# Norm sums of the mixers as wide float32r products, with root and reciprocal on 128x512 tiles

## What is computed

```python
# recurrence: o is (B, S, 4 heads, 128); the mean runs over the 128 values of a head
o = o * lax.rsqrt(jnp.mean(o * o, axis=-1, keepdims=True) + EPS)
o = o.reshape(bsz, s, A_WIDTH) * norm_g.astype(f32) * jax.nn.silu(g.astype(f32))

# attention: o is (B, S, 512); the mean runs over all 512 values of a token
return rmsnorm(o, norm_g).astype(q.dtype)
```

## Time and profile before

| | |
|---|---|
| median of 3 runs | 2477.68 us (2477.02 to 2479.18) |
| span of the profiled execution | 2476.5 us |
| TensorE busy | 2442.7 us, 99% |
| VectorE busy | 1336.4 us, 54% |
| ScalarE busy | 859.4 us, 35% |
| GpSimd busy | 254.0 us, 10% |

### The profile page before, as it was taken

How to read it: one execution, slowest core, us unless ns; L and a number is a source line. 1 busy time by engine, 2 the same in 40 slices (tenths; PEclk the granted TensorE clock), 3 DMA queues, 4 the chain that set the end, 5 groups by cost and what they waited for, 6 DMA issues and landing times.

```text
span 2476.5 us, 33433 instructions
## 1 busy us (share of the span) xinstructions
PE 2442.7 (99%) x11896; PEld 2022.3 (82%) x11896; DVE 1336.4 (54%) x2063; ACT 859.4 (35%) x1325; POOL 254.0 (10%) x237
## 2 busy tenths in 40 slices
PE   6999999999999999999999999999999999999998
PEld 5888888888888888888888888888888888888887
DVE  4665544555666554545556655455556665545433
ACT  4444422233344432223334453222334444222211
POOL 1220100000122100000012220000002122000000
PEclk9999999999999999999999999999999999999999
DMA  4222333333322233333331223333333223333332
GB/s 111 68 69 77 95 101 93 107 104 103 111 64 75 77 102 93 96 107 111 96 117 52 77 86 94 101 93 103 108 104 111 58 73 92 94 101 93 93 94 85
DMA packets 400998, 228.39 MB, mean 92 GB/s; under 512 B 11648, under 2 KB 388480, under 8 KB 400896
## 3 DMA queue, kind: packets, MB, share of 16 engines
q1 hardware_dynamic: 398592, 218.68, 29.8%
q10 hardware_dynamic: 2304, 8.39, 0.8%
HBM read 218.65 MB, written 8.39 MB: 92 GB/s over the span
## 4 chain that ended last, share of the span: by engine, by line
PE 97%; DMA 1%; DVE 1%; SPq 0%; issue 0%; ACT 0%; ACTq 0%; DVEq 0%
PE M L462 27%; PE M L464 27%; PE M L463 27%; PE X L544 2%; PE M L566 1%; PE X L607 1%; PE X L462 1%; PE X L463 1%; PE X L464 1%; PE X L620 1%; PE X L555 1%; PE X L480 1%; PE X L590 1%; PE X L469 1%; PE X L614 1%; DMA xs<-in_x_dram 1%
## 5 line engine op out<-in xcount | busy, mean ns | idle before, releaser
L1088 DVE TENSOR_TENSOR wlo<-raw,whi 128x1024 fp32r<-128x1024 f32 (+1 forms) x392 | 477.2, 1217 | 975.7 <-ACT whi L793 975.7
L462 PE MATMUL M<-uhi,whi 128*128 128x512 f32 x2112 | 833.7, 395 | 5.4 <-issue 3.8
L464 PE MATMUL M<-uhi,wlo 128*128 128x512 f32 x2112 | 823.9, 390 | 0.0
L463 PE MATMUL M<-ulo,whi 128*128 128x512 f32 x2112 | 823.6, 390 | 0.0
L793 ACT ACTIVATE whi<-raw 128x1024 fp32r<-128x1024 f32 (+1 forms) x392 | 408.5, 1042 | 1089.8 <-PE M L464 1079.9
L462 PEld LDWEIGHTS M<-uhi,whi 128*128 128x128 f32 x2112 | 397.3, 188 | 90.2 <-issue 9.1
L464 PEld LDWEIGHTS M<-uhi,wlo 128*128 128x128 f32 x2112 | 397.2, 188 | 84.2
L463 PEld LDWEIGHTS M<-ulo,whi 128*128 128x128 f32 x2112 | 397.7, 188 | 81.3 <-issue 1.0
L462 PE MATMUL M<-ahi,whi 128*128 128x512 f32 x832 | 331.4, 398 | 0.0
L464 PE MATMUL M<-ahi,wlo 128*128 128x512 f32 x832 | 328.4, 395 | 0.0
L463 PE MATMUL M<-alo,whi 128*128 128x512 f32 x832 | 328.3, 395 | 0.0
(11 more groups left out here) (175 smaller groups left out, 2164.5 us busy)
## 6 DMA issues: line engine op xcount, KB each, us to landing
raw<-in_w_in_dram SPq DMA_DIRECT2D x88, 512.0 KB, 3.9
raw<-in_w_gate_dram SPq DMA_DIRECT2D x88, 512.0 KB, 3.8
raw<-in_w_up_dram SPq DMA_DIRECT2D x88, 512.0 KB, 3.8
raw<-in_w_down_dram SPq DMA_DIRECT2D x64, 512.0 KB, 3.6
raw<-in_w_out_dram SPq DMA_DIRECT2D x32, 512.0 KB, 3.6
raw<-in_w_down_dram SPq DMA_DIRECT2D x32, 384.0 KB, 3.1
xs<-in_x_dram SPq DMA_DIRECT2D x32, 256.0 KB, 4.1
out_dram<-os ACTq DMA_DIRECT2D x16, 512.0 KB, 2.6
```

The lines of the kernel that those rows point to most:

```text
L462: mm(bank, whi[s][:, kb, :], hi, start=first, stop=False)
L463: mm(bank, whi[s][:, kb, :], lo, start=False, stop=False)
L464: return mm(bank, wlo[s][:, kb, :], hi, start=False, stop=last)
L1088: V.tensor_tensor(wlo[s][:, 0:nb, :], raw[s][:, 0:nb, :], whi[s][:, 0:nb, :].bitcast(F32), ALU.subtract).then_inc(s_lo[s], 1)
```

## The change

The two forms of the norm product are replaced. The squares are split in a high part (a float32r copy by ScalarE) and a low part (the difference, by VectorE), and two float32r products of a 128x128 tile of ones with them leave each token's sum on all 128 partitions of the bank: `sums_wide`. Nothing has to be spread any more. Root and reciprocal therefore work on 128x512 instead of 128x4, into `sqo` for the heads and `sroot` for the attention, and the factor is read from SBUF by the product with `gate` or `oT`. For a head the root stays in its slot and the reciprocal moves to the start of the next, before the product. For the attention the parts are made in slot 21 and sums, root and reciprocal stand in slot 22. The parts lie on memory that is free at that time (`gu`, `qT[1]`, `qT[2]`).

```diff
-            def spread(bank, factors, done):
-
-                for b in range(TB):
-                    last = mm(bank[:, b * P:(b + 1) * P], factors[:, b:b + 1].broadcast_to([P, P]), ident[:, :],
-                              start=True, stop=True)
-                last.then_inc(done, 1)
+            def sums_wide(bank, hi, lo, done):
+
+                mm(bank[:, :], ones_r[:, :], hi[:, :], start=True, stop=False)
+                mm(bank[:, :], ones_r[:, :], lo[:, :], start=False, stop=True).then_inc(done, 1)
...
             def head_sum(it, a):
-                pe.wait_ge(s_sq, it * HEADS + a + 1)
+                pe.wait_ge(s_sqlo, it * HEADS + a + 1)
                 pe.wait_ge(s_st, it * NCH * HEADS + NCH * a + NCH)
-                sums(X[3], sqo, s_asum)
-
-            def head_mul(it, a):
-                pe.wait_ge(s_arr, it * HEADS + a + 1)
-                spread(X[3], hrnrm, s_amul)
+                sums_wide(X[3], sqh, sql, s_asum)
...
-                    if slot == SWA_SUM:
-                        pe.wait_ge(s_oacc, it * (PAIRS - 1) + PAIRS - 1)
-                        sums(X[1], qT[0], s_ssum)
                     if slot == SWA_MUL:
-                        pe.wait_ge(s_srr, it + 1)
-                        spread(X[1], srnrm, s_smul)
+                        pe.wait_ge(s_sslo, it + 1)
+                        sums_wide(X[1], ssh, ssl, s_ssum)
...
             def output(it, a):
-                act.wait_ge(s_o, it * HEADS + a + 1)
+                n = it * HEADS + a
+                act.wait_ge(s_o, n + 1)
                 if a:
-                    act.wait_ge(s_asum, it * HEADS + a)
+                    act.wait_ge(s_ya, n)
                 A(sqo[:, :], X[2][:, :], ACT.Square).then_inc(s_sq, 1)
+                act.wait_ge(s_sq, n + 1)
+                A(sqh[:, :], sqo[:, :], ACT.Copy).then_inc(s_sqhi, 1)
...
-                A(hnrm[:, :], X[3][:, 0:TB], ACT.Sqrt, scale=1.0 / P, bias=epst[:, 0:1]).then_inc(s_aroot, 1)
+                A(sqo[:, :], X[3][:, :], ACT.Sqrt, scale=1.0 / P, bias=epst[:, 0:1]).then_inc(s_aroot, 1)
...
                     if slot == SWA_SUM:
+                        act.wait_ge(s_oacc, it * (PAIRS - 1) + PAIRS - 1)
+                        A(ssh[:, :], qT[0][:, :], ACT.Copy).then_inc(s_sshi, 1)
+                    if slot == SWA_MUL:
                         act.wait_ge(s_ssum, it + 1)
-                        A(snrm[:, :], X[1][:, 0:TB], ACT.Sqrt, scale=1.0 / (PAIRS * P),
+                        A(sroot[:, :], X[1][:, :], ACT.Sqrt, scale=1.0 / (PAIRS * P),
                           bias=epst[:, 0:1]).then_inc(s_sroot, 1)
...
+            def square_lo(it, a):
+                n = it * HEADS + a
+                dve.wait_ge(s_sqhi, n + 1)
+                if a:
+                    dve.wait_ge(s_asum, n)
+                V.tensor_tensor(sql[:, :], sqo[:, :], sqh[:, :].bitcast(F32), ALU.subtract).then_inc(s_sqlo, 1)
+
+            def head_mul(it, a):
                 n = it * HEADS + a
                 dve.wait_ge(s_aroot, n + 1)
-                if a:
-                    dve.wait_ge(s_amul, n)
-                V.reciprocal(hrnrm[:, :], hnrm[:, :]).then_inc(s_arr, 1)
-
-            def head_mul(it, a):
-                n = it * HEADS + a
-                dve.wait_ge(s_amul, n + 1)
+                V.reciprocal(sqo[:, :], sqo[:, :]).then_inc(s_arr, 1)
+                dve.wait_ge(s_arr, n + 1)
                 dve.wait_ge(s_y1, n + 1)
-                V.tensor_tensor(gate[a % 2][:, :], gate[a % 2][:, :], X[3][:, :], ALU.mult).then_inc(s_ya, 1)
+                V.tensor_tensor(gate[a % 2][:, :], gate[a % 2][:, :], sqo[:, :], ALU.mult).then_inc(s_ya, 1)
...
                     if slot == SWA_SUM:
+                        dve.wait_ge(s_sshi, it + 1)
+                        V.tensor_tensor(ssl[:, :], qT[0][:, :], ssh[:, :].bitcast(F32), ALU.subtract).then_inc(s_sslo, 1)
+                    if slot == SWA_MUL:
                         dve.wait_ge(s_sroot, it + 1)
-                        V.reciprocal(srnrm[:, :], snrm[:, :]).then_inc(s_srr, 1)
-                    if slot == SWA_MUL:
-                        dve.wait_ge(s_smul, it + 1)
+                        V.reciprocal(sroot[:, :], sroot[:, :]).then_inc(s_srr, 1)
+                        dve.wait_ge(s_srr, it + 1)
                         swa_mul(it, 0)
...
-                    for offset, step in ((KEYS, keys), (UPDATE, update), (OUTPUT, output), (NORM_SUM, head_sum)):
+                    for offset, step in ((KEYS, keys), (UPDATE, update), (OUTPUT, output), (OUTPUT, square_lo)):
```

More of the change, by code:

```diff
@@ L172, in block_program @@
         state = sb("state", [P, HEADS, P])
+        gu_at = (nc.sbuf_base + 31) // 32 * 32
         gu = [sb(f"gu{i}", [P, T]) for i in range(2)]
+        sqh, sql = (nc.alloc_sbuf_tensor_at(f"sq_part{i}", [P, T], F32R, offset=gu_at + 4 * T * i) for i in range(2))
         dist = sb("dist", [P, 2 * BLOCK])
@@ L177, in block_program @@
         ones = sb("ones", [P, P])
+        ones_r = sb("ones_r", [P, P], F32R)
         causal = sb("causal", [P, P])
@@ L215, in block_program @@
         gate = [tile(f"gate{i}") for i in range(2)]
+        q_at = free_tiles[:PAIRS]
         qT = [tile(f"qT{i}") for i in range(PAIRS)]
+        ssh, ssl = (nc.alloc_sbuf_tensor_at(f"ss_part{i}", [P, T], F32R, offset=q_at[1 + i]) for i in range(2))
+        sroot = qT[3]
         pr = [tile(f"pr{i}") for i in range(2)]
@@ L289, in block_program @@
         s_oacc = sem("s_oacc")
+        s_sshi = sem("s_sshi")
+        s_sslo = sem("s_sslo")
         s_ssum = sem("s_ssum")
@@ L292, in block_program @@
         s_srr = sem("s_srr")
-        s_smul = sem("s_smul")
         s_yb = sem("s_yb")
@@ L323, in block_program @@
         s_y1 = sem("s_y1")
+        s_sqhi = sem("s_sqhi")
+        s_sqlo = sem("s_sqlo")
         s_asum = sem("s_asum")
@@ L326, in block_program @@
         s_arr = sem("s_arr")
-        s_amul = sem("s_amul")
         s_ya = sem("s_ya")
@@ L347, in block_program @@
         s_osb = sem("s_osb")
-        INI, DST = 10, 4
+        INI, DST = 11, 4
         block = ctx.enter_context(nc.Block())
@@ L671, in slots @@
                             key_turn(it, HEADS - 1)
-                    a = head_at(slot, NORM_MUL)
-                    if a is not None:
-                        head_mul(it, a)
                     a = head_at(slot, UPDATE)
@@ L1241, in swa_mul @@
                 V.scalar_tensor_tensor(out=oT[p][:, :], in0=oT[p][:, :], scalar=gb[:, p:p + 1],
-                                       in1=X[1][:, :], op0=ALU.mult, op1=ALU.mult).then_inc(s_yb, 1)
+                                       in1=sroot[:, :], op0=ALU.mult, op1=ALU.mult).then_inc(s_yb, 1)
             def swa_lo(it, p):
@@ L1458, in _ @@
             G.memset(causal[:, :], -1.0).then_inc(s_ini, 1)
+            G.memset(ones_r[:, :].bitcast(F32), 1.0).then_inc(s_ini, 1)
             G.iota(dist[:, :].bitcast(I32), [[1, 2 * BLOCK]], base=-BLOCK, channel_multiplier=-1).then_inc(s_ini, 1)
-            pool.wait_ge(s_ini, 7)
+            pool.wait_ge(s_ini, 8)
             G.affine_select(out=causal[:, :], in_=causal[:, :], compare_op=ALU.is_ge, fill=0.0, base=0,
@@ L1465, in _ @@
             G.tensor_copy(dist0[:, :], dist[:, :].bitcast(I32)).then_inc(s_ini, 1)
-            pool.wait_ge(s_ini, 9)
+            pool.wait_ge(s_ini, 10)
             G.memset(causal[0:CHUNK, CHUNK:P], 0.0).then_inc(s_ini, 1)
@@ L1478, in _ @@
             pool.wait_ge(s_dst, 4)
-            pool.wait_ge(s_ini, 10)
+            pool.wait_ge(s_ini, 11)
             def copy(out, in_):
```

5 lines of the change are left out of this document (removed).

## The result

The changed kernel takes 2493.44 us (median of 4 runs, 2490.63 to 2497.53); the kernel before, on the same chip, 2477.80 (2477.02 to 2479.18). The ratio is 1.0062, with a 95% interval of 1.0048 to 1.0076: slower, by 15.6 us, where 22.8 were forecast. The profiled execution took 2490.63 us, its span is 2488.8 (12.3 more than before) and its mean granted clock 0.989, where the kernel before had 0.997.

What follows compares the result with a forecast made beforehand. TensorE's own work was taken to bound the kernel, busy 2442.7 of 2476.5 us. Savings of 26.8, waits of 4 x 9.4 and clock of 12.0 gave +22.8 us: 2500.5 us, range 2485 to 2508.

Steps and rivals of the forecast that it cites:

- What is taken off TensorE: Norm sums and spreading: two float32r products replace them, saving 1.34 us per norm, 6.7 per superblock, 26.8 in all.
- Rival (c): Product with ones runs in several passes like fp32, so the savings fall: about 2520 us; chance 0.02.
- Root and reciprocal: On 128x512 the root takes 0.67 us and the reciprocal 3.35; each norm's way to its factor grows by over 3.
- Rival (b): Wide reciprocal is short enough, under 2.45 us; at 1.75 us the kernel takes 2472.1; chance 0.10 with its neighbours.
- nothing late at all: Limit given under rival (b): no result comes late for TensorE, 2450.9 us.
- Heads 0 and 1: Slots 11 and 16: TensorE's keys step waits for GpSimd's `key`, 0.45 us each, 0.9 per superblock.
- Head 2: Slots 20 and 21: TensorE's turn of head 3's `iv` waits for head 2's gate product, idling 3.5 us per superblock.
- the attention norm: Slots 22 and 23: state steps queue behind the reciprocal, so TensorE's output step idles 3.4, with weight load 3.5 us.
- The table load's row: ScalarE's activation starts as soon as the load's 1.28 us are over, so a drain of 1.38 us was left out.
- The tail: Slots 24 to 26: x's seventh turn waits for its DMA, 1.5 us per superblock, bounds 0.6 and 3.
- The clock: Falls behind the two 3.5 us gaps, 1.7 us each, less 0.4: +3.0 per superblock, +12.0 in all.
- Rival (a): The waits come but the clock holds: +10.8, 2488.5 us; chance 0.28.

Runs made afterwards that it cites:

- the arena's place held: Changed kernel with the tile of ones behind the arena and 128 unused bytes ahead of it, so the arena lies where it lay before: 2511.02 us, ratio 1.0126.
- short-reciprocal run: Changed kernel with both reciprocals done on 4 of the 512 columns, the other columns keeping the root: 2443.95 us, ratio 0.9860.
- early request: In the version put together, third and fourth piece of x asked for one and two weight units earlier: 2447.71 us; without that, 2450.76 us.
- filler run: Changed kernel with 15 and 14 unneeded 128x512 products per superblock issued on TensorE in the two long waits: 2469.74 us, ratio 0.9970.
- version put together: Changed kernel with heads 0 to 2's reciprocals later in VectorE's queue, old attention norm, head 3's turn waiting for the root, x asked for earlier: 2447.71 us.

## Why the prediction was right or wrong

The direction, the mechanisms and the places were right; the result lies in the range. The distance of 7 us is the rest of three errors: +12 us of clock that I didn't count, -15.6 us of placement that I didn't see, and 3.2 us of waits too many in the sum, 2.5 of them in the tail. That the result lies in the range is luck in part: with the arena's place held the change measured 2511.0, above the 2508 at which the range ends.

**What is taken off TensorE.** Right. The sums start at 111.61 and the next group at 112.18, 0.57 us for the pair; its first step takes 0.34, which spares the group's own first step 0.09 (0.32 before, 0.23 now), so 0.48 stands for the 0.46 of the sum. The spreading is gone. The run with the place held fixed bears the saving out: there the savings (-26.8), the waits (34.2 less the 0.8 of before, +33.4) and the clock (half of the 54.0 us in which TensorE worked at half clock, less the 1.7 of before, +25.3) make +31.9, and 33.6 was measured. Rival (c), several passes, is out:

```profile
L476 PE MATMUL X<-sq_part,ones_r 128*128 128x512 f32 x16 | 6.3, 394 | 0.0
```

**Root and reciprocal.** Right: 3353 ns for the heads', where the 3346 of the earlier trace rows stood in. Rival (b) hung on this price being under 2.45 us. The short-reciprocal run shows what it would have brought: 2443.95, or 2459.6 with the arena's 15.6 us added back. That is above the 2450.9 of "nothing late at all", since waits of 7.4 us are left, where the kernel before had 0.8.

**Heads 0 and 1.** The size was right, the second place was not. For head 0:

```profile
117.25 3.35 DVE L1229 RECIPROCAL sqo<-sqo 128x512 f32<-128x512 f32 x1
...
125.99 1.58 POOL L1499 TENSOR_TENSOR key<-key,cuminv 128x512 f32<-128x512 f32 x1 [6.67 <-DVE cuminv L1177]
...
127.63 1.16 PE L595 MATMUL X<-qdec,key 128*128 128x128 f32 x8 [0.38 <-POOL key L1499]
```

The other wait I had given to `key` too. It came a step earlier and from another result: the product with `vals` needs bank M[3], whose last content VectorE copies to `oT` behind the reciprocal. It took 0.53 us and left none for `key`. Together 0.9 a superblock, as in the sum.

```profile
172.15 0.67 PE L571 MATMUL M<-pT,vals 128*64 128x128 f32 x8 [0.53 <-DVE oT L1300]
```

**Head 2** (3.5 forecast, 3.48 measured) **and the attention norm** (3.4 to 3.5 forecast, 3.37 measured). Right to a tenth. The table load's row had it that the activation starts as soon as the 1.28 us are over. That holds: load at 204.24, root at 205.53, so 1.29, and 1.30 at 221.25. Ahead of the two loads ScalarE's last instruction ends 0.02 and 0.01 us before them. The drain of about 1.38 us that the Trainium skill, "ScalarE: Activation LUTs", section "What ACT_TABLE_LOAD costs", would add showed in neither, and the forecast with it (+5.5) would have been farther off.

**The tail.** The mechanism was right, the term too large: 1.5 forecast, 1.1 measured (4.3 us in four superblocks, over the 0.8 of before: +0.9 each, 3.5 in all where the sum had 6.0), and split over two turns, 0.86 and 0.28 in the first superblock. The early request takes it away, as said above.

**The clock.** This is the step that failed in size. "Each fall costs half of 3.4" took a stretch of 3.4 us from the only row inside the dense part. Behind the new waits the stretches were 3.4 to 10.2 us, mostly 6.8. The last row (after a wait of 3.2 us) shows 4.2 us of such a stretch, which in the trace of before goes on to 6.8 (2464.1 to 2470.9); I used it for whether the clock falls and not for how long it stays down. The whole came to 23.7 us by the filler run and about 22 by the short reciprocal, where 12.0 stood in the sum. How often was nearly right: seven of eight. By the rule of the Trainium skill, "TensorE: Matmul & The Clock Gate", section "Why this matters for your kernels", all eight should have fallen; one of the same length did not, and nothing in the trace says why. It is not tied to that place: in the run with the arena's old place, with the same instructions and waits, all eight fell, and with the state steps ahead of the reciprocal it was the fourth superblock's wait in slot 21 (3.47 us) that cost nothing. Rival (a), the clock holds, lies nearer to the result than the forecast (5 us off, against 7), but for the wrong reason: with the arena's place held, the change gives 2511, and the filler run refutes a clock that costs nothing.

**What no step had.** The prediction took "the groups' own products" as untouched. Their count and form were; their pace was not. Nothing that I read in the trace of before could have priced this, but one thing could have been seen: its groups of the same form had 395 ns in one operand and 390 in the other, a difference of 1.3% on over a quarter of TensorE's work (2880 products of 233 ns) with no explanation, and the diff moved that operand's tile.

## What to carry to other kernels

On a kernel whose TensorE is busy to 99%, work taken off it is only gained if every result it needs still comes in time: a long operation put into another engine's queue delays all that is queued behind it, and taking away one wait hands it to the next queue that the operation holds, until the operation itself is moved. Price a new wait with the slow stretch behind it, which here cost nearly as much as the wait, and test that price by filling the gap. When an edit changes the sizes of tiles, compare the pace of products that it doesn't touch, and hold the place fixed in one experiment before you explain the rest.

## What was not expected of the hardware

- The pace of the large 128x512 float32r products follows the distance between the tiles of the two operands: 227 ns where it is an even multiple of 128 bytes, 232 to 233 where it is odd, in seven layouts. Why is open. An unused tile of 384 bytes was worth 0.7% of this kernel.
- In the stretch shown the clock fell some 2 us into the wait, in others only after it had ended, and half rate lasted 3.4, 6.8 or 10.2 us by the records, behind waits of nearly one length (2.7 to 3.5 us). One wait of 3.49 us in eight was followed by none, and in the version put together one of 1.06 us was followed by 3.4 us of it.
- 116 needless products made a kernel 23.7 us faster.
